# First norm, pooling, attention outputs and the order of the attention groups, changed together in a diffusion trunk kernel

## The chip, the cores and the metric

One core of a Trainium2 chip runs the whole program. The metric is the device time of one execution in microseconds (us); a profile is one more execution, taken with the hardware profiler. TensorE does the matrix products and transposes, VectorE, ScalarE and GpSimd the rest, and SP does nothing but issue transfers between DRAM and SBUF, in the order of its own list and waiting on semaphores. VectorE is DVE in the rows, ScalarE ACT, GpSimd POOL, TensorE PE, and its weight loads PEld.

## The reference

A step of a diffusion backbone of two layers, on 128 context tokens and 1024 latent tokens of width 1024. What the change touches lies in layer 0, up to its output projection. In short:

```python
ada = silu(cond) @ w_ada[l] + b_ada[l]            # per layer; cond is c (latent) or c_ctx (context)
sh1, sc1, g1, sh2, sc2, g2 = split(ada, 6)
u = layer_norm(x) * (1 + sc1) + sh1
proj = u @ w_in                                   # q: 8 heads of 64, k and v: 2 heads, p: 512 channels
q, k = rms_norm(q, q_g), rms_norm(k, k_g)         # rotary on the latent tokens
attn = block_attention(q, k, v)                   # context reads context; latent reads latent and cached keys
pool = pool_mixer(p, w_pool, pool_scale)          # per group: (centred mean over 2/4/8/16 tokens - p) @ w_pool
x = layer_norm(alpha * x + g1 * (concat(attn, pool) @ w_out), ln_g, ln_b)
u = layer_norm(x) * (1 + sc2) + sh2
f = conv_ffn(u, w_up, conv, w_down)
x = layer_norm(alpha * x + g2 * f, ln_g, ln_b)
```

Layer 1 has a convolution and a Fourier mixer instead of attention and pooling.

## The kernel before

Every engine's list is written out by hand, and semaphores (named in `wait_ge` and `then_inc`) set the order between engines. Values that go into matrix products are kept in two parts, a rounded high part (made by ScalarE, `copy`, L870) and the rest as a low part (made by VectorE, `lo`, L1357, a subtraction); a product is three passes. The 1152 tokens are nine tiles of 128, the first of them the context. `act_a` and `act_b` hold activations with channels on the partitions.

**The modulation vectors (w_ada).** Each layer's 6 x 1024 columns are cut into halves of 512, *blocks*; `ada_half` (L89) says which block is which. Blocks 0 to 12 are early, 13 to 23 late. SP loads an early block in four pieces of 512 KB into the six slots of `ada_w` (`ada_units`, L463, each piece waiting for its slot's `ada_used`), `ada_block` (L1860) multiplies it with the conditions. Blocks 0 to 3 go to `ada_top` by ScalarE (`top_evac`, L889), and `top_cols` (L1885) turns them into the first shift and scale (`cols`). Blocks 4 to 12 go to `ada_row` by VectorE (`ada_evac`, L1401), and GpSimd stores them to DRAM (L748 to L756). Late blocks come through `late_w` (`late_units`, L473; the fifth piece waits for the ninth z_rdy), `late_block` on TensorE (L1870), `late_evac` on ScalarE (L894) and the same loop of stores on GpSimd.

**First norm, "in".** `ln_steps` (L393) runs eleven steps, each of them with tile s - 1 in its normalisation and tile s - 2 in its rounding. VectorE's step (`ln_vec`, L1409): statistics, reciprocal, the split of `act_a` (which raises act_rdy), `ada_evac` of block 4 + s. ScalarE's step (`ln_act`, L913): eight `ln_u` activations that apply shift and scale to the transposed tile (L939), the square root (L952), `ln_z` = normalised tile (L968), the copy to `act_a` (`rounding`). TensorE's step (`ln_turns`, L2016): block 4 + s, then eight transposes of `ln_z` into banks 6 and 7 (`ln_turn`), and ahead of tile 5's the first pooling product `chunk(0, 0)` (L2007). There is one `ln_z`, so the normalising of a tile waits for the transposes of the one before. SP (`ln_loads`) loads x three tiles ahead into `ln_y`, each behind z_rdy of the tile that leaves its slot.

**SP's order.** Blocks 0 to 2; two units of the pooling weights (`u_unit`, into `raw_u`, split later to `uw`); block 3; three tiles of x; block 4; two more units of raw_u; two of wq (`d_unit`, through `raw_d`); blocks and x of the norm; block 13; `bias_rows` (L485), which waits for `ada_stored` and for the ninth act_rdy and then reads the stored rows back; then wq, late blocks and wkv in turn.

**Pool projection and pooling.** TensorE runs `pool_chunk` for four groups and three thirds (`NCH` 3), with late blocks between them; results go to `pp`. GpSimd pools the four windows over it (L758 to L785), each a chain of passes over 1173 columns, after all of `bank_free` and after `brow_mm` 6.

**q, k, v.** `qkv` (L2055) of the nine tiles, with `turn_keys` (L2067) for the keys of each tile, which waits for VectorE's rotated k. The mixer product, `mix` (L2083), has 12 parts in three banks, each evacuated by `mix_out` on ScalarE; the first three stand ahead of the last tile's `turn_keys`, the others between the first group's peaks.

**Attention.** `Group` (L409) n is one tile of queries with one kv head; groups 0 and 1 are the context's (one block of keys, one turn of scores), 2 to 17 the sample's (nine blocks, three turns). Group n + 1's maxima are prepared while group n's scores run: `turn_queries`, four `peak_scores` (three matmuls of 384 columns each for a sample group, one of 128 for a context group), VectorE's `maximum`, `turn_peaks`. Then `scores`, ScalarE's exponentials and rounding, GpSimd's p_low (L814), and `weigh_high` and `weigh_low` into bank 6 + n % 2. Outputs: `outputs` copies the sums (ScalarE), four `o_inverse` (VectorE), `o_scale` (L1545) writes the scaled outputs from the bank to `o_f` and raises o_mul, `o_round` (ScalarE) and `o_split` (L1554, raises m_att) put them into `act_b`. `weigh_high` of group n waits for o_mul of group n - 2, whose bank it takes. Behind the last group come `wo`'s parts (`wo_hi`, `wo_lo`), the low parts of the mixed channels (`mixed_lo`) and the gate rows (`mid_gate`, L1926).

## Time and profile before

| what | us |
|---|---|
| time, median of 3 runs | 2843.91 (2843.7 to 2844.75) |
| the profiled execution: its time | 2844.56 |
| the profiled execution: its span | 2843.0 |
| TensorE busy (matmuls) | 2680.5, 94% |
| TensorE's weight loads | 2386.7, 84% |
| VectorE busy | 1530.3, 54% |
| ScalarE busy | 921.4, 32% |
| GpSimd busy | 433.3, 15% |

The span runs from the first instruction to the last; the execution's own time has 1.56 us around it. TensorE is busy nearly all the time, but a busy share is an average over stages. By the trace the first norm ends at 123.3 us (the ninth act_rdy), the q/k/v stage runs from 210.7 to 304.7 us, the first scores start at 326.5 us, the attention's groups follow each other every 14 us, and the output projection starts at 575.3 us.

### The profile page before, as it was taken

How to read it: one execution, taken by the hardware profiler on the slowest of the kernel's cores; microseconds unless marked ns; L12 is line 12 of the kernel's file. 1: busy time of each engine (PE TensorE's matmuls, PEld its weight loads, DVE VectorE, ACT ScalarE, POOL GpSimd, SP SyncE). 2: the span in 40 equal slices, each digit the busy share in tenths (PEclk: the TensorE clock that was granted, in tenths of full speed). 3: DMA queues.
4: the chain of work that ended last, by engine and by line, in shares of the span. 5: the costliest groups of instructions: out<-in, count | busy, mean ns of one | idle time of the engine just before them, and what ended most of it. 6: DMA issues, size and time to landing. Idle time of an engine off the chain costs nothing.

```text
span 2843.0 us, 36166 instructions
## 1 busy us (share of the span) xinstructions
PE 2680.5 (94%) x13884; PEld 2386.7 (84%) x13884; DVE 1530.3 (54%) x2157; ACT 921.4 (32%) x1402; POOL 433.3 (15%) x258
## 2 busy tenths in 40 slices
PE   5698799999899999999997899999899999999997
PEld 1477577768899999999996899978899999999996
DVE  1315588856555555555557433247555555555557
ACT  2521377745322222222225511136322222222223
POOL 1116187825000000000006100014000000000003
PEclk6799899999999999999999899999999999999999
DMA  9770100022311111111012212122311111110112
GB/s 329 275 267 6 62 1 1 1 90 82 126 45 44 44 44 44 44 37 44 30 37 74 74 41 71 59 90 82 126 45 44 44 44 44 37 44 30 42 32 82
DMA packets 171518, 196.08 MB, mean 69 GB/s; under 512 B 7625, under 2 KB 125877, under 8 KB 171439
## 3 DMA queue, kind: packets, MB, share of 16 engines
q1 hardware_dynamic: 169748, 194.33, 20.7%
q8 instruction: 53, 0.87, 0.1%
q0 software_dynamic: 1280, 0.33, 0.1%
q10 hardware_dynamic: 411, 0.34, 0.0%
q14 instruction: 26, 0.21, 0.0%
HBM read 175.64 MB, written 19.33 MB: 69 GB/s over the span
## 4 chain that ended last, share of the span: by engine, by line
PE 84%; DVE 6%; ACT 4%; issue 2%; DMA 2%; POOL 1%; SPq 0%; ACTq 0%; POOLq 0%; DVEq 0%
PE ps L2011 47%; PE ps L2230 18%; PE ps L1978 5%; PE ps L1961 2%; PE ps L2121 1%; PE ps L2157 1%; ACT ln_u L939 1%; PE ps L2142 1%; PE ps L2143 1%; PE ps L2063 1%; PE ps L2164 1%; DVE stats L1391 1%; DMA ada_w<-in_w_ada 1%; DVE small L1538 1%; PE ps L1923 1%
## 5 line engine op out<-in xcount | busy, mean ns | idle before, releaser
L2011 PE MATMUL ps<-act_b,uw 128*128 128x384 f32 x4608 | 808.0, 338 | 7.7 <-DVE act_b L1357 6.2
L2011 PEld LDWEIGHTS ps<-act_b,uw 128*128 128x128 f32 x4608 | 804.2, 189 | 9.5 <-DVE act_b L1357 6.8
L2011 PEld LDWEIGHTS ps<-act_a,uw 128*128 128x128 f32 x3456 | 605.2, 190 | 17.5 <-issue 9.2
L2011 PE MATMUL ps<-act_a,uw 128*128 128x384 f32 x3456 | 611.7, 339 | 6.8 <-DVE act_a L1357 5.3
L2230 PE MATMUL ps<-dw,hh 128*128 128x512 f32 x2112 | 502.7, 398 | 9.0 <-DVE acc L1651 9.0
L2230 PEld LDWEIGHTS ps<-dw,hh 128*128 128x128 f32 x2112 | 398.1, 189 | 108.7 <-DVE acc L1651 10.1
L1651 DVE TENSOR_TENSOR acc<-acc,ps 128x512 f32<-128x512 f32 x360 | 245.7, 686 | 215.1 <-PE ps L2230 215.1
L870 ACT ACTIVATE fa<-ps 128x384 f32<-128x384 f32 (+2 forms) x176 | 67.3, 410 | 839.0 <-PE ps L2011 839.0
L1357 DVE TENSOR_TENSOR uw<-raw_u,uw 128x1024 fp32r<-128x1024 f32 x112 | 136.6, 1221 | 121.3 <-ACT uw L870 118.0
L1612 DVE TENSOR_SCALAR ft<-fa,fgrp 128x1153 f32<-128x1153 f32 x44 | 38.7, 880 | 299.2 <-ACT fa L870 284.1
L814 POOL TENSOR_TENSOR p_low<-p_exp,p_top 128x1536 fp32r<-128x1536 f32 (+1 forms) x50 | 170.7, 3418 | 75.8 <-ACT p_top L870 75.3
L1681 DVE TENSOR_TENSOR fh<-ft,ps 128x384 f32<-128x384 f32 (+2 forms) x176 | 73.9, 450 | 168.4 <-PE ps L2011 160.7
L853 POOL TENSOR_TENSOR acc<-acc,gb_end 128x1024 f32<-128x1024 f32 x9 | 21.3, 2375 | 822.0 <-ACT acc L1217 822.0
L870 ACT ACTIVATE uw<-raw_u 128x1024 fp32r<-128x1024 f32 x112 | 117.8, 1053 | 66.3 <-PE ps L2011 66.2
L846 POOL TENSOR_SCALAR acc<-acc,stats 128x1024 f32<-128x1024 f32 x9 | 10.8, 1198 | 806.5 <-DVE stats L1399 806.5
L870 ACT ACTIVATE hh<-fh 128x384 fp32r<-128x384 f32 x132 | 66.5, 520 | 205.6 <-DVE fh L1681 205.6
L827 POOL TENSOR_TENSOR ln_y<-ln_y,gbm 128x1024 f32<-128x1024 f32 x18 | 43.5, 2417 | 424.3 <-ACT ln_y L948 424.3
L939 ACT ACTIVATE ln_u<-ps,cols 128x128 f32<-128x128 f32 x216 | 78.3, 467 | 87.9 <-PE ps L1923 77.7
L1538 DVE TENSOR_REDUCE small<-ps 128x1 f32<-128x1152 f32 (+1 forms) x72 | 88.5, 1230 | 15.2 <-PE ps L2121 13.4
L1196 ACT ACTIVATE ft<-ft 128x1153 f32<-128x1153 f32 x44 | 51.5, 1171 | 132.7 <-DVE ft L1614 126.8
L1068 ACT ACTIVATE p_exp<-ps 128x1536 f32<-128x1536 f32 (+1 forms) x50 | 71.0, 1421 | 38.8 <-PE ps L2143 38.8
L1357 DVE TENSOR_TENSOR hh<-fh,hh 128x384 fp32r<-128x384 f32 x132 | 73.2, 555 | 17.4 <-ACT hh L870 11.9
(208 smaller groups left out, 3135.9 us busy)
## 6 DMA issues: line engine op xcount, KB each, us to landing
raw_u<-in_w_up SPq DMA_DIRECT2D x88, 512.0 KB, 4.0
ada_w<-in_w_ada SPq DMA_DIRECT2D x52, 512.0 KB, 6.5
late_w<-in_w_ada SPq DMA_DIRECT2D x44, 512.0 KB, 6.5
raw_d<-in_w_down SPq DMA_DIRECT2D x44, 512.0 KB, 3.7
raw_u<-in_w_in_odd SPq DMA_DIRECT2D x20, 512.0 KB, 3.8
ln_y<-in_x_all SPq DMA_DIRECT2D x18, 512.0 KB, 5.1
xs<-ln_y SPq DMA_DIRECT2D x18, 512.0 KB, 2.6
acc<-xs SPq DMA_DIRECT2D x6, 1536.0 KB, 11.6
```

The costliest lines, as they stand in the source:

```text
L814: gp.tensor_tensor(p_low[:, s % 3, 0:nb, :], p_exp[:, s % 2, 0:nb, :], p_top[:, s % 3, 0:nb, :].bitcast(F32), ALU.subtract).then_inc(p_lo, 1)
L870: return act.activation(o, i, ACT.Copy)
L939: o = act.activation(ln_u[:, k * P:(k + 1) * P], ps[:, 6 + k // 4, (k % 4) * P:(k % 4 + 1) * P], ACT.Identity, bias=cols[:, l, c0, k, cc:c ...
L1068: act.activation(p_exp[:, s % 2, 0:nb, :], ps[:, 3:3 + nb, :], ACT.Exp).then_inc(exp_done, 1)
L1357: return v.tensor_tensor(dst, src, hi.bitcast(F32), ALU.subtract)
L1538: v.tensor_reduce(g.peak(h), ps[:, 0:nb, 0:nw], mybir.AxisListType.XY, ALU.max, negate=True).then_inc(mx_done, 1)
L1651: return v.tensor_tensor(a, a, ps[:, 6 + j % 2, :], ALU.add).then_inc(down_added, 1)
L1681: o = v.tensor_tensor(f_h[l][:, s0:s0 + ln], f_t[l][:, p0:p0 + ln], ps[:, 3 + c, s0 - c * CH:s0 - c * CH + ln], ALU.mult)
L1961: mm = pe.matmul(ps[:, 2 * tile + h, :], src[:, k, a, tile * P:(tile + 1) * P], wo[l][:, k, w, 512 * h:512 * (h + 1)], start=n == 0 and (a ...
L1978: mm = pe.matmul(ps[:, 2 * (tile % 3) + h, :], src[:, k, a, tile * P:(tile + 1) * P], wo[l][:, k, w, 512 * h:512 * (h + 1)], start=(k, a, ...
L2011: mm = pe.matmul(out, uw[:, u_slot, w, k, :], src[:, k, a, c * CH:(c + 1) * CH], start=(k, w, a) == (0, 0, 0), stop=(k, w, a) == (KD - 1, ...
L2230: mm = pe.matmul(ps[:, 6 + h, :], hh[l][:, b, a, tile * P:(tile + 1) * P], w_[:, b, w, 512 * h:512 * (h + 1)], start=(b, a, w) == (0, 0, 0 ...
```

## The change

**Group order.** Places 0, 1, 2 hold groups 2, 0, 1; from place 3 on nothing moves. Slots and banks go by place. `outputs()` is the half of the group's bank in which the scaled outputs are kept.

```diff
-            def __init__(self, g):
+            def __init__(self, place):
+                g = (2, 0, 1)[place] if place < 3 else place
                 self.g, self.kv, self.ctx, self.q = g, g % 2, g < 2, g // 2 - 1
                 self.nk = 1 if self.ctx else LKB
                 self.key0 = LAT + PAST if self.ctx else 0
                 self.sizes = [1] if self.ctx else [TRI] * (LKB // TRI)
-                self.s0 = g if self.ctx else 2 + (g - 2) * (LKB // TRI)
+                self.s0 = (0, LKB // TRI, LKB // TRI + 1)[place] if place < 3 else 2 + (place - 2) * (LKB // TRI)
                 self.last = len(self.sizes) - 1
-                self.slot = g % 2
-                self.bank = 6 + g % 2
+                self.slot = place % 2
+                self.bank = 6 + place % 2
...
+
+            def outputs(self):
+                return ps[:, self.bank, :].rearrange("p (a h t) -> p a h t", h=2, t=P)[:, :, self.kv, :]
```

**First norm, loads.** x of the first three tiles comes between the first blocks, the blocks 11 and 12, two units of raw_u and two of wq behind the norm's loads; block 4 + tile stands behind its tile's transposes, and the halves that the blocks 4 to 10 hold are exchanged. The x load of tile + 3 waits for the transposes (zt_done) and no longer for z_rdy; so does late block 13's fifth piece.

```diff
+MIX_EARLY = 7
...
-    if m < 7:
-        return 1, m - 4
-    if m < 13:
-        return 0, m - 3
-    return (1, 3) if m == 13 else (0, m - 4) if m < 16 else (1, m - 12)
+    if m == 4:
+        return 1, 0
+    if m < 11:
+        return 0, m - 1
+    return (1, m - 10) if m < 14 else (0, m - 4) if m < 16 else (1, m - 12)
...
-    return {s: [4 + s] for s in range(9)} if kind == "in" else {}
+    return {s: [s + 2] for s in range(2, 11)} if kind == "in" else {}
...
-        ada_row = at("ada_row", [P, 3, 512], F32, off_s + 28672)
+        ada_row = at("ada_row", [P, 6, 512], F32, off_s + 24576)
+        ada_side = at("ada_side", [P, 3, 512], F32, off_s + 12288)
```
```diff
-                        sp.wait_ge(z_rdy, NT)
+                        sp.wait_ge(zt_done, NT)
...
+            def first_x(s):
+                sp.dma_start(ln_y[:, s, :], dram_rows(t["x_all"], s)).then_inc(x_ld[s], 16)
+
+            ada_units(0)
+            ada_units(1)
+            first_x(0)
+            ada_units(2)
+            ada_units(3)
+            first_x(1)
+            first_x(2)
+            ada_units(4)
             for n in range(2):
                 u_unit(n, u_source(n))
-            ada_units(3)
-            for s in range(3):
-                sp.dma_start(ln_y[:, s, :], dram_rows(t["x_all"], s)).then_inc(x_ld[s], 16)
-            ada_units(4)
...
-                            sp.wait_ge(z_rdy, tile + (NT * i4 + 1))
+                            sp.wait_ge(zt_done if i1 is None else z_rdy, tile + (NT * i4 + 1))
...
-                        for m in ada_steps(kind).get(3 + j, []):
-                            ada_units(m, i)
+                        if i1 is None:
+                            ada_units(5 + j, i)
...
-            for n in range(2, 4):
-                u_unit(n, u_source(n))
-            for k in range(2):
-                d_unit(D_QKV + k, t["w_in_even"][0][k * P:(k + 1) * P, 0:AW], AW)
             ln_loads("in", t["x_all"])
+
             def wq_unit(k):
                 d_unit(D_QKV + k, t["w_in_even"][0][k * P:(k + 1) * P, 0:AW], AW)
+
+            ada_units(11)
+            ada_units(12)
+            u_unit(2, u_source(2))
+            u_unit(3, u_source(3))
+            wq_unit(0)
+            wq_unit(1)
```

**First norm, ScalarE and VectorE.** The normalised tile is written over `ln_y`; there is no `ln_z` in it. The copy to `act_a` stands ahead of the normalising; the normalising of a tile and the rounding of the tile two before share a step.

```diff
-            ln_act("in", act_a)
+            def first_norm(s):
+
+                if s.live(2):
+                    tile = s.tile(2)
+                    cc = 1 if s.first(2) else 0
+                    if s.first(2):
+                        act.wait_ge(cols_done, 2)
...
+                    for k in range(KD):
+                        o = act.activation(ln_u[:, k * P:(k + 1) * P], ps[:, 6 + k // 4, (k % 4) * P:(k % 4 + 1) * P],
...
+                st, y = stats[:, s.slot(0), :], ln_y[:, s.slot(0), :]
+                if s.live(0):
+                    act.wait_ge(stat2, s.tile(0) + 1)
+                    act.activation(st[:, 34:35], st[:, 33:34], ACT.Sqrt, bias=eps, scale=1.0).then_inc(sd2, 1)
+                if s.live(2):
+                    tile = s.tile(2)
+                    act.wait_ge(mod_done, tile + 1)
+                    copy(act_a[:, :, 0, bass.ds(tile * P, P)], ln_u[:].rearrange("p (k t) -> p k t", k=KD)).then_inc(act_hi, 1)
+                if s.live(0):
+                    act.wait_ge(rs2, s.tile(0) + 1)
+                    act.activation(y, y, ACT.Identity, bias=st[:, 36:37], scale=st[:, 35:36]).then_inc(z_rdy, 1)
+                if s.i is None and s.base == 0:
+                    top_evac(2)
+                    top_evac(3)
+                elif s.i is None and s.base == 2:
+                    for n in range(2):
+                        u_hi_at(n, 0, n)
+
+            ln_steps(act, first_norm)
 
```
```diff
+                used = ADA_SLOTS + 4 * m + 4
                 v.wait_ge(ada_used, used if i is None else i * 12 + used)
-                if turn:
-                    v.wait_ge(ada_st[slot], 32 * turn if i is None else i * 32 + 32 * turn)
-                v.tensor_copy(ada_row[:, slot, :], ps[:, 3 + m % 3, :]).then_inc(ada_bank, 1)
+                if i is not None:
+                    row = ada_row[:, bass.ds(i * 3 + (m - 5), 1), :].rearrange("p a n -> p (a n)")
+                else:
+                    row = ada_side[:, (4, 11, 12).index(m), :]
+                v.tensor_copy(row, ps[:, 3 + m % 3, :]).then_inc(ada_bank, 1)
...
+            def first_norm(s):
+
+                if s.live(0):
+                    tile, st = s.tile(0), stats[:, s.slot(0), :]
+                    v.wait_ge(x_ld[s.slot(0)], s.third(0) * 16 + 16)
+                    norm_stats(ln_y[:, s.slot(0), :], st, 20).then_inc(stat2, 1)
+                    v.wait_ge(sd2, tile + 1)
+                    norm_scale(st, 20).then_inc(rs2, 1)
+                for m in ada_steps("in").get(s.base, []):
+                    ada_evac(m, s.i)
+                if s.live(2):
+                    tile = s.tile(2)
+                    v.wait_ge(act_hi, tile + 1)
+                    lo(act_a[:, :, 1, bass.ds(tile * P, P)], ln_u[:].rearrange("p (k t) -> p k t", k=KD), act_a[:, :, 0, bass.ds(tile * P, P)]).then_inc(act_rdy, 1)
+                if s.i is None and s.base < 2:
+                    cols_of(range(s.base, s.base + 1))
+                elif s.i is None and s.base == 2:
+                    u_lo_at(0, 0, 0)
+                    u_lo_at(1, 0, 1)
...
-                    o = v.tensor_tensor(o_f[HD * odd:HD * odd + HD, :, :],
+                    o = v.tensor_tensor(g.outputs()[HD * odd:HD * odd + HD],
...
-                lo(act_b[:, blocks, 1, cols_], o_f[:], act_b[:, blocks, 0, cols_]).then_inc(m_att, 1)
+                lo(act_b[:, blocks, 1, cols_], g.outputs(), act_b[:, blocks, 0, cols_]).then_inc(m_att, 1)
```

**Rows and pooling.** GpSimd stores the early rows only (there is a row buffer for each); ScalarE issues the stores of the late rows. Each pooling window starts with its own group's `bank_free`; only the last waits for `brow_mm` 6.

```diff
+                l, half = ada_half(m)
                 e = m - ADA_LATE
                 act.wait_ge(ada_used, ADA_SLOTS + 4 * m + 4)
                 if e >= 2:
                     act.wait_ge(late_st[e % 2], 32 * (e // 2))
                 copy(late_row[e % 2][:], ps[:, 6 + m % 2, :]).then_inc(ada_bank, 1)
+                act.wait_ge(ada_bank, m + 4)
+                for c in range(2):
+                    act.dma_start(ada[l, c::2, half * 512:half * 512 + 512], late_row[e % 2][c::32, :]).then_inc(late_st[e % 2], 16)
...
-            for m in range(ADA_TOP):
+            for m in range(2):
                 top_evac(m)
-            for n in range(2):
-                u_hi_at(n, 0, n)
```
```diff
-            for m in range(ADA_TOP, ADA_ALL):
+            for m in range(ADA_TOP, ADA_LATE):
                 l, half = ada_half(m)
+                rows = ada_side[:, (4, 11, 12).index(m), :] if m in (4, 11, 12) else ada_row[:, m - 5, :]
                 gp.wait_ge(ada_bank, m + 4)
-                if m < ADA_LATE:
-                    rows, done = ada_row[:, (m - ADA_TOP) % 3, :], ada_st[(m - ADA_TOP) % 3]
-                else:
-                    rows, done = late_row[(m - ADA_LATE) % 2][:], late_st[(m - ADA_LATE) % 2]
...
+                    gp.dma_start(ada[l, c::2, half * 512:half * 512 + 512], rows[c::32, :]).then_inc(ada_st[(m - ADA_TOP) % 3], 16)
+
+            gp.wait_ge(u_split, 2 + U_FFN0)
             for g, w in enumerate(WINDOWS):
 
+                gp.wait_ge(bank_free[g % 2], 3 * (g // 2 + 2))
+                if g == NPG - 1:
+                    gp.wait_ge(brow_mm, 6)
+                    for a in range(2):
+                        o = gp.memset(vv[:, :, a, 1, :].bitcast(F32), 1.0 - a)
+                    o.then_inc(v_one, 1)
```

**Mixer and TensorE.** Seven mixes stand ahead of the last tile's `turn_keys`, with their `mix_out` on ScalarE ahead of the last tile's k rounding. `weigh_high` and the first gate wait for m_att.

```diff
             pe.wait_ge(setup_c, 2)
-            for m in range(ADA_TOP):
-                ada_block(m)
-            top_cols()
+            for n in range(2):
+                ada_block(2 * n)
+                ada_block(2 * n + 1)
+                top_cols(n)
+            pe.wait_ge(cols_done, 2)
...
+                z = ln_z if i4 else ln_y[:, tile % 3, :]
                 pe.wait_ge(z_rdy, NT * i4 + tile + 1)
...
-                    mm = pe.transpose(ps[:, 6 + k // 4, (k % 4) * P:(k % 4 + 1) * P], ln_z[:, k * P:(k + 1) * P], ident)
+                    mm = pe.transpose(ps[:, 6 + k // 4, (k % 4) * P:(k % 4 + 1) * P], z[:, k * P:(k + 1) * P], ident)
...
-                        pe.wait_ge(o_mul, NGR)
+                        pe.wait_ge(m_att, NGR)
...
-                for s in range(NT + 1):
-                    for m in ada_steps(kind).get(s, []):
-                        ada_block(m)
-                    if s == 6:
+            def first_turns(next_chunk):
+
+                for tile in range(NT):
+                    if tile == 5:
                         next_chunk(0)
-                    if s:
-                        ln_turn(s - 1, LN[kind]["i4"])
-                    if s == NT:
-                        next_chunk(1)
+                    ln_turn(tile, 0)
+                    ada_block(ADA_TOP + tile)
+                next_chunk(1)
...
-            for m in range(3):
+            for m in range(MIX_EARLY):
                 mix(m)
...
-                    pe.wait_ge(o_mul, n - 1)
+                    pe.wait_ge(m_att, n - 1)
...
             turn_queries(0)
-            mix(3)
             for h in range(G):
                 peak_scores(0, h)
-                mix(4 + 2 * h)
-                mix(5 + 2 * h)
+                mix(MIX_EARLY + h)
+            for m in range(MIX_EARLY + G, NPG * NCH):
+                mix(m)
```

On ScalarE `mix_out` moves into the last tile of `qkv_tile` (`MIX_EARLY` of them), the last two tiles leave the loop, and `o_round` reads `g.outputs()`.

## Rows read from the trace of the kernel before

**Rows 1.** Windows by stage: stretch, us, busy us (x instructions), clock, DMA share, GB/s.
```profile
123.30:210.70 87.40, 78.60 (x481) 57.91 (x473) 10.34 (x17) 19.20 (x38) 12.37 (x22) 0.91 0.81 281
210.70:305.00 94.30, 84.92 (x452) 72.86 (x452) 54.35 (x103) 15.60 (x51) 47.42 (x45) 0.92 0.02 6
361.50:558.00 196.50, 195.32 (x911) 156.26 (x910) 169.48 (x169) 152.61 (x141) 156.72 (x69) 1.00 0.00 1
```
**Rows 2.** The same windows over three stretches of the first norm.
```profile
0.00:16.00 16.00, 4.92 (x24) 1.54 (x28) 0.00 (x0) 3.43 (x5) 4.29 (x6) 1.00 0.70 229
16.00:98.40 82.40, 54.84 (x280) 23.58 (x272) 25.73 (x56) 35.19 (x71) 8.05 (x14) 0.67 1.02 360
108.00:124.00 16.00, 10.29 (x52) 8.82 (x56) 6.94 (x12) 12.41 (x27) 1.12 (x2) 0.63 0.03 9
```
**Rows 3.** Waits of SP's queue up to 130 us: total us, times, longest us.
```profile
SPq L488 <- DVE act_a L1357: 22.2, 1, 22.2
```
**Rows 4.** Timeline of ScalarE and VectorE, a turn of the norm loop: start, us, instruction.
```profile
95.57 0.68 DVE L1407 COPY ada_row<-ps 128x512 f32<-128x512 f32 x1
...
96.32 2.90 ACT L939 ACTIVATE ln_u<-ps,cols 128x128 f32<-128x128 f32 x8 [2.15 <-PE ps L1923]
...
99.89 1.24 ACT L968 ACTIVATE ln_z<-ln_y,stats 128x1024 f32<-128x1024 f32 x1 [0.48 <-DVE stats L1399]
...
103.58 2.90 ACT L939 ACTIVATE ln_u<-ps,cols 128x128 f32<-128x128 f32 x8 [1.51 <-DVE act_a L1357]
```
**Rows 5.** DMA issues: count, KB each, median us from issue to landing.
```profile
ada_parts<-ada_row POOLq DMA_DIRECT2D x18, 8.0 KB, 4.9
```
**Rows 6.** Waits of TensorE from 124 to 305 us.
```profile
PE ps L2072 <- DVE k L1357: 9.4, 5, 4.4
...
PE ps L1881 <- DMA late_w<-in_w_ada: 7.4, 4, 4.0
```
**Rows 7.** Timeline of TensorE in the first norm.
```profile
90.97 4.44 PE L2011 MATMUL ps<-act_a,uw 128*128 128x384 f32 x24
```
**Rows 8.** GpSimd and VectorE in time from 246 us, and a group of instructions by form.
```profile
246.82 7.43 POOL L772 TENSOR_TENSOR pool_t<-pool_t 128x1173 f32<-128x1173 f32 x3
...
249.24 2.49 DVE L1503 TENSOR_TENSOR xn<-xn,g_row 128x512 f32<-128x512 f32 x1
...
L1503 DVE TENSOR_TENSOR xn<-xn,g_row 128x512 f32<-128x512 f32 x5 | 3.4, 681 | 0.0
```
**Rows 9.** The windows once more, behind TensorE's longest wait for k.
```profile
258.00:263.50 5.50, 5.50 (x19) 4.79 (x20) 2.78 (x7) 1.62 (x5) 3.18 (x2) 0.54 0.06 15
```
**Rows 10.** Timeline of TensorE, from the first query transposes to the third group's weighing.
```profile
314.82 1.09 PE L2108 MATMUL ps<-con,q_two 128*128 128x128 f32 x4 [0.61 <-ACT kt L870]
...
326.48 0.47 PE L2142 MATMUL ps<-q_top,kt 128*128 128x512 f32 x1 [0.50 <-ACT q_low L870]
...
346.66 0.76 PE L2142 MATMUL ps<-q_top,kt 128*128 128x512 f32 x1
...
361.49 0.39 PE L2142 MATMUL ps<-q_top,kt 128*128 128x512 f32 x1
...
367.48 1.56 PE L2157 MATMUL ps<-p_top,vv 128*128 128x512 f32 x6
```
**Rows 11.** Timeline of VectorE in the attention, its start and its end.
```profile
338.38 1.36 DVE L1538 TENSOR_REDUCE small<-ps 128x1 f32<-128x1152 f32 x1
...
339.65 0.94 DVE L1543 RECIPROCAL o_inv<-o_raw 64x128 f32<-64x128 f32 x1
...
362.41 1.72 DVE L1357 TENSOR_TENSOR act_b<-o_f,act_b 128x256 fp32r<-128x256 f32 x1
...
569.04 3.76 DVE L1357 TENSOR_TENSOR act_b<-o_f,act_b 128x256 fp32r<-128x256 f32 x1 [2.29 <-ACT act_b L870]
```
**Rows 12.** Timeline of GpSimd at the end of the attention.
```profile
565.59 6.93 POOL L814 TENSOR_TENSOR p_low<-p_exp,p_top 128x1536 fp32r<-128x1536 f32 x2 [0.17 <-ACT p_top L870]
```
**Rows 13.** Groups of VectorE's instructions by form, 361 to 558 us: busy us, mean ns, idle.
```profile
L1357 DVE TENSOR_TENSOR q_low<-ps,q_top 64x512 fp32r<-64x512 f32 x14 | 9.6, 682 | 2.6 <-ACT q_top L870 1.8
```

More of the change, by code:

```diff
@@ L1043, in _ @@
             qkv_tile(0, 0, True)
-            with act.Fori(0, NQ // 2) as i:
+            with act.Fori(0, NQ // 2 - 1) as i:
                 for j in range(2):
                     qkv_tile(i * 2 + (j + 1), 1 - j, False)
+            qkv_tile(NQ - 1, 1, False)
+            qkv_tile(NQ, 0, False, last=True)
             def q_round(n):
@@ L1444, in step @@
                         lo(dest[:, :, 1, bass.ds(tile * P, P)], ln_u[:].rearrange("p (k t) -> p k t", k=KD), dest[:, :, 0, bass.ds(tile * P, P)]).then_inc(act_rdy, 1)
-                    for m in ada_steps(kind).get(s.base, []):
-                        ada_evac(m, s.i)
                 def loop(i):
@@ L1456, in from_psum, with first_loop @@
                 return 2, ps[:, 2 * slot:2 * slot + 2, :]
-            ln_vec("in", act_a, None)
+            def first_norm(s):
[16 more added lines that the diff above has]
+                    u_lo_at(1, 0, 1)
+            def first_loop(i):
+                if i is None:
+                    chain.leave(2)
+                else:
+                    chain.enter(i, 6)
+            ln_steps(v, first_norm, first_loop)
             for n in range(NPG):
@@ L2095, in mix @@
                 mm.then_inc(mix_done, 1)
-            for m in range(3):
+            for m in range(MIX_EARLY):
                 mix(m)
```

75 lines of the change are left out of this document (27 added, 48 removed).

## Prediction

> **What bounds the kernel now.** I read the windows by stage first, to see which engine fills each stretch. From 361.5 us the groups run with TensorE busy 195.3 of 196.5 us [rows 1]; the work after the attention is untouched. So what VectorE, ScalarE or GpSimd save in the attention's steady part is worth nothing, and only the stretch before 361.5 us and the seam behind the attention can move the end. Next come the windows of the transfers. The queue is full from 16 us on: by 98.4 us it has moved 33.3 MB (16 x 0.229 + 82.4 x 0.360), and from 108 to 124 us it stands almost still [rows 2]. The waits of SP say why: 22.2 us for the last split of act_a [rows 3]. That is `bias_rows`, which waits for the ninth act_rdy (123.3 us); all later loads are queued behind it on SP. And act_rdy is late because a turn of the norm loop takes 7.26 us, from the first ln_u of a tile (96.32) to that of the next (103.58), with ln_z (1.24 us), the copy to act_a and its split one after the other [rows 4]. Then the pool stage has TensorE busy 78.6 of 87.4 us, and the q/k/v stage 84.9 of 94.3 [rows 1], of which 9.4 us are waits for VectorE's k [rows 6].
>
> **Part 1, the first norm (up to q/k/v).** Removed: the single ln_z. The norm is written back into ln_y, so ScalarE's copy to act_a comes ahead of the next normalising, and VectorE's split runs beside that. Of the 7.26 us the 1.24 us of ln_z and some 0.3 us of handover leave the chain: about 5.7 us a tile. That is less than the 7.3 us that a tile's loads need (four pieces of w_ada and one tile of x, 2.62 MB, at 0.360 MB/us [rows 2]). So the transfers are late next, and the sum goes by bytes. The last act_rdy now needs what stands ahead of its split in VectorE's list, ada_evac(12), and so all 13 early blocks: 27.3 MB of w_ada, 4.7 MB of x, 1.0 MB of raw_u and 0.4 MB of constants, 33.4 MB together. The queue of before has moved that at 98.4 us; the other two units of raw_u, two of wq and the four pieces of block 13 now come behind it. One hole is new: x(tile+3) waits on SP for the transposes of its tile, and TensorE does `chunk(0, 0)`, 4.44 us [rows 7], ahead of tile 5's. Queued on SP behind that wait are x8, the blocks 10 to 13, raw_u and wq. I charge 3 us, between nothing (pieces in flight cover it) and 4.4. Block 12 is through TensorE about 1 us after landing, at 102.4. Its copy (0.68 us [rows 4]) and GpSimd's store, which lands 4.9 us after its issue [rows 5], let SP pass `ada_stored` at about 109; the act_rdy, a copy and a split behind the block, is earlier and no longer decides. Against 123.3 that is -14.3 us.
>
> The pool stage behind it is the same list on TensorE, and TensorE is its bound, so it moves as a whole. Its 7.4 us of waits for late_w [rows 6] stay: block 14 is still asked for after `bias_rows`. Two costs are added. The 22 stores of the late rows are issued by ScalarE behind its own late_evac; the copies of wq, wkv and pp are queued behind them, and ScalarE is busy 19.2 of 87.4 us [rows 1]: nothing to 1 us. And GpSimd's windows 0 to 2 now run beside VectorE's splits of wq and wkv. A two-operand instruction took 2.49 us beside GpSimd where its kind takes 681 ns undisturbed [rows 8]; the loads of wkv and of block 22 are queued on SP behind such splits. Bounds 0 and 5 us, for up to three that meet a pass; I take 1.3 for both additions, near to one blocked instruction, since the splits are few. Part 1: **-13 us**, between -18 (no hole, rows stored in time) and -6 (the larger additions and a second hole).
>
> **Part 2, q/k/v.** The pooling leaves this stage except for window 3, which still waits for bank 1 and brow_mm and ends some 18 us into the stage (three of its passes are the 7.43 us [rows 8]). VectorE's rotation of the first tiles then runs alone. Of the 9.4 us of waits [rows 6] the first keeps about 1 us (the chain of the cached keys) and the rest, some 0.2 us each, another 1: 7.4 go. Behind the longest wait the granted clock is 0.54 from 258 to 263.5 us [rows 9], (1 - 0.54) x 5.5 = 2.5 us lost, and I put 1 us to the shorter ones. That makes 10.9; the end of window 3 may still touch the first tile: **-10**, between -6 and -12.5.
>
> Here a rule is weighed. The row shows q_low<-ps, whose first operand is in PSUM, at 682 ns beside GpSimd through the whole attention [rows 13], while instructions with two SBUF operands stand still for whole passes. The Trainium skill, "SBUF — State Buffer", section Who interferes with whom, has the same split as a rule: the port pair is an exclusive lock, the second comer blocks fully, and an instruction with at most one SBUF input stays out of it. It speaks against the move of the pooling: what the lock cost in q/k/v it can cost in the pool stage. By the rule with every such split late the sum would be the second rival's, by the rows of before, whose pool stage has no GpSimd arithmetic, the forecast.
>
> **Part 3, the mixer and the order of the groups.** Seven mixes instead of three fill TensorE's wait for the last tile's k; ScalarE evacuates them ahead of that tile's k_round, on which the last keys wait, and has time for it: nothing. Five mixes are left, but the first four peaks are now a full group's. From the first transposes (314.82) to the first scores (326.48) it was 11.7 us [rows 10]. A full head's reduction takes 1.36 us [rows 11] and its three matmuls stand in the open, so by estimate each head takes 0.85 us more: 15.1 us, +3.4. Then three groups. Before, from 326.48 over 346.66 to 361.49 [rows 10], 35.0 us: two short groups with one full set of peaks in the open, 20.2, and a full group, 14.8. Now: a full group over short peaks, held by GpSimd's p_low (two are 6.93 us [rows 12]), 13; a short group whose maxima alternate with four reciprocals of 0.94 us [rows 11] and wait for the full group's last p_low, 10; a short group with the next full peaks in the open, 14 of the 20.2. 37 us, +2. The order exposes one more set of full peaks. With half clock behind the waits I take **+6**, between -1 (only the saved mixes count) and +9.
>
> **Part 4, outputs in their bank.** o_f goes; o_scale writes PSUM and o_split reads it. In the steady part VectorE saves about a microsecond a group, which TensorE hides. Added is that the bank is free at m_att, not at o_mul: `weigh_high` two groups on waits for o_round and o_split, and the peaks, scores and weights behind it on TensorE with it. The split (362.41, 1.72 us [rows 11]) is 3.3 us ahead of that weigh_high (367.48 [rows 10]): 0. At the seam the split at 569.04 stands 3.76 us [rows 11] beside GpSimd's last p_low; read from PSUM it doesn't. But mixed_lo, next on VectorE and with two SBUF operands, meets the same p_low, so only the split's own time comes off: **-0.4**, between 0 and -1.7. The gate behind k = 2 waits for m_att too; the split stands right behind the wo_lo that k = 2 needs: 0.
>
> **Sum.** -13 - 10 + 6 - 0.4 = -17.4 us on the profiled execution's 2844.56: 2827.2. The median of the runs is 0.65 lower: **2826.5**.
>
> **Rivals.** First: the order costs nothing. For it speaks that mixes fill the full peaks' gaps, against it that five mixes are fewer than the nine of before. Part 3 is 0: 2820.5. Second: the lock moves. Windows 0 to 2 meet the splits of wq and wkv, SP is held, late blocks 22 and 23 come late; part 1 is -6: 2833.5. For it speaks the 2.49 us row, against it VectorE's 10.3 busy us in the 87.4 [rows 1]. Third: the stores don't hold SP and no hole comes; part 1 is -18: 2821.5. Fourth, on the other side: the queue runs dry in every tile, since x(tile+3) now waits for TensorE's transposes and all blocks stand behind it. Where each of the five x loads other than the chunk's loses 4.4 us, 22 us are added: 2848.5; it is a loss from 3.5 us a load. Against it speaks that a tile's chain (5.7 us) is shorter than its bytes (7.3). Fifth, the same sign: the later release of the bank stops TensorE. If m_att comes 2 us behind `weigh_high` in 14 groups, 28 us are added: 2854.5; it decides from 1.2 us a group, beyond the 3.3 us of slack.
>
> **How the numbers follow.** Chances: forecast 0.47, first rival 0.20, second 0.12, third 0.12, fourth 0.05, fifth 0.04. About 0.2% (5.7 us) is what a measurement of this kernel can tell from no change. Faster by more (under 2838.2) are the forecast, the first, the third and most of the second rival: 0.88. Same: the edges of the forecast and of the second, 0.06. Slower: the rest, 0.06. The range goes from 2812 (parts 1 to 3 at -18, -12.5 and -1) to 2838 (part 1 at -6 with part 3 at +9 and part 2 at -9), which leaves the last two rivals out.
>
> **What the profile after would show.** Right: the ninth act_rdy at about 105, SP held by the stores and not by act_a, q/k/v from about 198 us, no wait for k over 1.5 us in it, the fourth group's scores some 17 us ahead of 361.5, groups still 14 us apart. Wrong: a queue with holes in every tile before 100 us, splits of wq or wkv of over 2 us, weigh_high idle for act_b, or the first scores less than 13 us behind the first transposes.

## The result and the profile after

The changed kernel takes 2826.76 us (median of 5 runs, 2819.72 to 2829.55), against 2843.91 before: a ratio of 0.9936, 95% interval 0.9921 to 0.995 (it is estimated from all runs of both kernels; the two medians alone give 0.994). The forecast was 2826.5. The total hides that two of its parts were off, in opposite directions. The table reads the traces by stage. Each border is the start of a row of the timeline: SP's read of the stored rows, the first q/k/v product, the keys of the last tile but one, the first query transposes, and the gate behind the third part of the output projection. The profiled execution of each kernel stands in it; the experiments in its lower rows are told below.

| kernel | read of rows at | to q/k/v | q/k/v | last keys | transposes to gate | gate to end |
|---|---|---|---|---|---|---|
| before | 123.34 | 87.35 | 94.00 | 10.13 | 272.95 | 2255.2 |
| after | 110.09 | 91.53 | 81.88 | 9.74 | 276.88 | 2255.0 |
| e1 order of before | 109.69 | 87.94 | 82.11 | 9.76 | 270.91 | 2255.0 |
| e2 pooling late | 110.65 | 85.58 | 93.16 | 9.74 | 276.30 | 2255.5 |
| e3 o_f back | 110.42 | 91.30 | 82.39 | 9.74 | 275.81 | 2253.1 |
| e4 block 13 ahead | 111.98 | 90.11 | 82.08 | 9.74 | 275.44 | 2253.4 |
| e5 context last | 108.67 | 90.55 | 83.29 | 9.94 | 270.33 | 2253.1 |
| e6 block 22 ahead | 112.64 | 85.83 | 82.08 | 9.75 | 276.67 | 2258.3 |
| e7 half blocks | 101.61 | 90.59 | 82.08 | 9.74 | 275.74 | 2253.3 |
| e8 e5 and e6 | 111.02 | 84.32 | 82.04 | 9.74 | 270.00 | 2255.4 |
| e9 e8 and the seam | 110.41 | 85.26 | 82.07 | 9.75 | 265.59 | 2253.0 |

Rows whose code is the same in a column show how far one execution stands from the next: 108.7 to 112.6 in the first column (before and e7 aside), 87.9 to 91.5 in the pool stage (after, e1, e3 and e5), 81.9 to 82.4 in q/k/v (e2 aside, and with e5 up to 83.3), 2253.0 to 2258.3 behind the gate, 275.4 to 276.9 from the transposes to the gate in the six with the changed order. A difference of a microsecond says something in the last keys, one of two in q/k/v and from the transposes to the gate; in the other columns one execution can't tell less than four or five. The medians of one kernel have the same scatter in them, so the experiments are judged by the stage that they touch, and by the ratio to the kernel before.

The windows of the changed kernel, in the columns of [rows 1]: the transfers up to 98.4 us, the pool stage, q/k/v.

```profile
16.00:98.40 82.40, 55.18 (x304) 26.15 (x296) 32.97 (x73) 48.70 (x97) 8.59 (x15) 0.75 0.99 354
110.09:201.62 91.53, 81.37 (x481) 59.85 (x481) 14.17 (x15) 19.20 (x36) 30.13 (x30) 0.89 0.77 271
201.62:283.50 81.88, 80.40 (x450) 68.90 (x449) 47.98 (x103) 15.50 (x51) 15.64 (x14) 0.98 0.03 7
```

The queue runs at 354 GB/s where it ran at 360 [rows 2]: by this rate the new waits of SP for transposes cost, as an estimate, 82.4 x (1 - 354/360) = 1.4 us of transfers. The last piece of block 12 came in at 101.6 all the same, 3.2 us behind 98.4: with units of raw_u and wq beside it the queue had moved 33.9 MB by then (101.6 x 0.334), not 33.4. The pool stage has 30.1 us of GpSimd in it where it had 12.4 [rows 1], all of that the issuing of stores, and VectorE is busy 3.8 us longer with the same 15 to 17 instructions. The q/k/v stage lost 31.8 us of GpSimd, and TensorE idles 1.5 us in it where it idled 9.4.

The ninth act_rdy is the split at 103.82; block 12 passes TensorE behind a wait for its last piece. The timeline of TensorE and VectorE:

```profile
101.59 1.43 PE L1926 MATMUL ps<-ada_w,conds 128*32 128x512 f32 x8 [2.03 <-DMA ada_w<-in_w_ada]
...
103.82 1.23 DVE L1398 TENSOR_TENSOR act_a<-ln_u,act_a 128x1024 fp32r<-128x1024 f32 x1
```

SP then stands for the store of block 12's row, and later for the splits of wq, as its waits from 108 us show (total us, times, longest us):

```profile
SPq L588 <- DVE wq L1398: 6.3, 2, 4.1
SPq L493 <- DMA ada_parts<-ada_side: 6.1, 1, 6.1
```

What [rows 3] showed, 22.2 us of SP before the last split of act_a, is gone; the store took its place with 6.1 us. TensorE's waits for k in the q/k/v stage, 9.4 us in [rows 6], fell to 1.4:

```profile
PE ps L2129 <- DVE k L1398: 1.4, 3, 1.1
```

In TensorE's timeline the rows that answer to [rows 10] are the first transposes at 293.24, the first scores at 307.20 and the fourth group's at 344.40 (314.82, 326.48 and 361.49 before):

```profile
293.24 1.03 PE L2165 MATMUL ps<-con,q_two 128*128 128x128 f32 x4 [0.56 <-ACT kt L878]
...
307.20 0.47 PE L2199 MATMUL ps<-q_top,kt 128*128 128x512 f32 x1 [0.34 <-ACT q_low L878]
...
344.40 0.77 PE L2199 MATMUL ps<-q_top,kt 128*128 128x512 f32 x1
```

### The profile page after: what moved, and what is told of

Its sections match the earlier page's. It is cut to its first block, busy times and chain, and to the rows that moved or that the text cites. A ratio compares the mean times of both kernels' runs of the same rounds, so it can differ in the third digit from the quotient of the medians.

```text
span 2825.1 us, 36154 instructions
## 1 busy us (share of the span) xinstructions
PE 2675.1 (95%) x13884; PEld 2384.5 (84%) x13884; DVE 1510.2 (53%) x2157; ACT 920.7 (33%) x1402; POOL 421.1 (15%) x236
## 4 chain that ended last, share of the span: by engine, by line
PE 82%; DVE 7%; ACT 4%; DMA 3%; issue 3%; POOL 1%; SPq 0%; ACTq 0%; POOLq 0%; DVEq 0%
PE ps L2072 47%; PE ps L2287 18%; PE ps L2039 5%; DMA ada_w<-in_w_ada 2%; DVE small L1598 2%; PE ps L2022 1%; PE ps L2120 1%; DVE stats L1428 1%; PE ps L2178 1%; ACT p_exp L1117 1%; PE ps L2199 1%; PE ps L2200 1%; DMA late_w<-in_w_ada 1%; PE ps L2221 1%; PE ps L1984 1%
## 5 line engine op out<-in xcount | busy, mean ns | idle before, releaser
L854 POOL TENSOR_SCALAR acc<-acc,stats 128x1024 f32<-128x1024 f32 x9 | 10.8, 1201 | 806.6 <-DVE stats L1436 806.6
L1603 DVE RECIPROCAL o_inv<-o_raw 64x128 f32<-64x128 f32 x72 | 67.1, 938 | 31.3 <-ACT o_raw L878 30.6
L1398 DVE TENSOR_TENSOR hh<-fh,hh 128x384 fp32r<-128x384 f32 x132 | 73.3, 555 | 17.4 <-ACT hh L878 12.0
## 6 DMA issues: line engine op xcount, KB each, us to landing
acc<-xs SPq DMA_DIRECT2D x6, 1536.0 KB, 12.4
```

What stands on the lines that cost most here:

```text
L1398: return v.tensor_tensor(dst, src, hi.bitcast(F32), ALU.subtract)
L1603: v.reciprocal(o_inv[g.out, cols_], o_raw[g.sum, cols_]).then_inc(inv_done, 1)
```

## The experiments

All are edits of the changed kernel.

**e1, the order of the groups as before.**

```diff
-                g = (2, 0, 1)[place] if place < 3 else place
+                g = place
-                self.s0 = (0, LKB // TRI, LKB // TRI + 1)[place] if place < 3 else ...
+                self.s0 = g if self.ctx else 2 + (g - 2) * (LKB // TRI)
```

> The changed kernel with the attention groups in the order of before (the two of the context first); seven early mixes and the rest stay. Theory (the order costs, because a full group's four peaks stand in the open twice): the first peaks are short again, so first transposes to first scores falls from 13.96 us to some 9 (four mixes fewer than before in it, where it was 11.7), and the first three groups from 37.2 to 35.0: about -7 us on the changed kernel's 2826.8, 2820. Rival (the order is free, since mixes fill the peaks and the short groups are held by p_low anyway): 2826 to 2828. Against both: if the sample's group first hides more than it shows, it is slower, 2830.

Measured: 2821.45 us, ratio 0.9924 (0.9909 to 0.9938). The first transposes to the first scores take 10.32 us:

```profile
289.50 0.63 PE L2165 MATMUL ps<-con,q_two 128*128 128x128 f32 x4 [0.57 <-POOL q_two L810]
...
299.82 0.47 PE L2199 MATMUL ps<-q_top,kt 128*128 128x512 f32 x1 [0.51 <-ACT q_low L878]
```

That is 3.6 us less than in the changed kernel, and from the transposes to the gate it is 6.0 us less (270.91 against 276.88; the five other kernels with the changed order have 275.4 to 276.7). The order costs; that it is free, the first rival, falls. Up to the start of the projection, ahead of a seam that is not the same in all of them (see e3), e1 takes 258.4 us and the six with the changed order 264.2 to 265.9. Against before (272.95) e1, with the early mixes alone, is 2.0 us shorter; so of part 3 the order is +5 to +7 and the mixes some -2, from one execution of e1 and of before.

**e2, the pooling windows behind the last bank and the columns, as before.**

```diff
             gp.wait_ge(u_split, 2 + U_FFN0)
+            gp.wait_ge(bank_free[0], 3 + 6)
+            gp.wait_ge(bank_free[1], 3 + 6)
+            gp.wait_ge(brow_mm, 6)
```

> The changed kernel with all four pooling windows where they were before, behind the last bank and the fifth and sixth columns. Theory (the port lock costs in both stages): q/k/v goes from 81.9 us back to about 94 (waits for k of 8 to 9 us, half clock behind the longest), and the pool stage, from the read of the stored rows (110.0) to the first q/k/v product (201.6), falls from 91.6 to about 89, because the splits of wq at 150 and 172 us (3.23 and 4.34 us for two) run undisturbed at 1.3 and block 22 is asked for 3 us earlier: +9, 2836. Rival (the late blocks are late because ScalarE issues the stores, not because of the lock): the pool stage stays at 91.6, +12, 2839.

Measured: 2834.64 us, ratio 0.9965 (0.9954 to 0.9975). The q/k/v stage is back at 93.2 us, with 10.8 us of waits for k, and the pool stage falls to 85.6. Here are the last two splits of wq and GpSimd's passes beside them (VectorE and GpSimd in time), TensorE's waits for block 22, and the window of the 32 products behind the second of these waits, first in the changed kernel:

```profile
171.04 4.69 POOL L780 TENSOR_TENSOR pool_t<-pool_t 128x1173 f32<-128x1173 f32 x2
...
171.94 4.34 DVE L1398 TENSOR_TENSOR wq<-raw_d,wq 128x512 fp32r<-128x512 f32 x2 [18.75 <-ACT wq L878]
...
182.42 1.06 PE L1941 MATMUL ps<-late_w,conds 128*32 128x512 f32 x8 [2.30 <-DMA late_w<-in_w_ada]
185.76 1.94 PE L1941 MATMUL ps<-late_w,conds 128*32 128x512 f32 x8 [2.28 <-DMA late_w<-in_w_ada]
...
185.70:193.49 7.79, 7.73 (x32) 5.85 (x32) 0.00 (x0) 0.60 (x1) 0.00 (x0) 0.67 0.89 321
```

then with the pooling late, and its row of SP's waits for wq:

```profile
173.31 1.29 DVE L1401 TENSOR_TENSOR wq<-raw_d,wq 128x512 fp32r<-128x512 f32 x2 [21.22 <-ACT wq L881]
...
182.03 1.06 PE L1944 MATMUL ps<-late_w,conds 128*32 128x512 f32 x8 [0.51 <-DMA late_w<-in_w_ada]
184.57 1.07 PE L1944 MATMUL ps<-late_w,conds 128*32 128x512 f32 x8 [1.47 <-DMA late_w<-in_w_ada]
...
184.57:189.93 5.36, 5.36 (x32) 4.27 (x32) 0.00 (x0) 0.60 (x1) 0.00 (x0) 1.00 1.03 374
...
SPq L588 <- DVE wq L1401: 3.2, 2, 3.0
```

Two splits that take 4.34 us together beside GpSimd take 1.29 without it, and SP's wait for wq falls from 6.3 to 3.2 us. ScalarE issues the late stores in both kernels, so it is the pooling, not the stores, that adds these 3.1 us. The pool stage pays 2 to 6 us for it (after, e1, e3, e4 and e5: 87.9 to 91.5, against 85.6), where I expected 2.6. By the Trainium skill, "SBUF — State Buffer", section Who interferes with whom, the shared port pair is an exclusive lock. By that rule two-operand splits had to stand still for GpSimd's passes here as they did in q/k/v, and these rows agree.

The waits for block 22 are 4.6 us in the changed kernel (3.8 to 5.0 in the six with the early pooling and block 22 behind wkv) and 2.0 here. The low clock comes on top: the 32 products behind the second wait have a granted clock of 0.67 and take 7.8 us (6.8 to 8.3 in the six), where they take 5.4 at 1.00 here. The last 32 small matmuls, 5.5 us at 0.65 against 3.7 at 1.00, don't follow the wait: in e1, with waits of 3.8 us, they take 3.7, and in e9, with none, 5.3.

**e3, outputs in SBUF again.**

```diff
-                    o = v.tensor_tensor(g.outputs()[HD * odd:HD * odd + HD],
+                    o = v.tensor_tensor(o_f[HD * odd:HD * odd + HD, :, :],
...
-                    pe.wait_ge(m_att, n - 1)
+                    pe.wait_ge(o_mul, n - 1)
```

> The changed kernel with the outputs in SBUF again (o_f, and o_mul where m_att was waited for). Theory (the bank pays at the seam alone): the steady groups stay at 14.0 us, the split of the last but one group stands beside GpSimd's p_low again (3.7 us instead of 0.42) and the gate behind the third part of the output projection comes 1.6 us later: 2828.4. Rival (the later release of the bank costs TensorE in the groups): the stretch from the fourth group to the projection falls from 214.8 us to 213.8 and the time is 2826 or below.

Measured: 2824.42 us, ratio 0.9932 (0.992 to 0.9945); transposes to gate 275.81. VectorE's groups by form over the steady groups (busy us, mean ns, idle), first of the changed kernel, then of this one:

```profile
L1398 DVE TENSOR_TENSOR act_b<-ps,act_b 128x256 fp32r<-128x256 f32 x16 | 6.5, 408 | 2.7 <-ACT act_b L878 2.7
```

```profile
L1399 DVE TENSOR_TENSOR act_b<-o_f,act_b 128x256 fp32r<-128x256 f32 x16 | 29.1, 1821 | 2.8 <-ACT act_b L879 2.8
```

The split is 1.4 us shorter from the bank, 22.6 us of VectorE in all, and the stage is not: neither theory holds at its price. The 1.6 us that the trace shows between the projection's start and the gate (10.95 against 12.51 before) are not the bank's, since e1 has the outputs in the bank and takes 12.54, and e3 has them not and takes 11.03. What changes is which products get the low clock. The windows of the first 24 and the next 12 products, in the changed kernel and then in e1:

```profile
559.17:566.54 7.37, 7.37 (x24) 5.60 (x24) 7.26 (x9) 0.84 (x3) 0.00 (x0) 0.77 0.76 257
567.16:570.10 2.94, 2.94 (x12) 2.17 (x12) 2.94 (x4) 2.17 (x4) 0.00 (x0) 1.00 0.95 308
```

```profile
547.87:553.63 5.76, 5.76 (x24) 4.43 (x24) 5.73 (x6) 0.19 (x1) 0.00 (x0) 1.00 0.69 207
555.87:560.40 4.53, 4.53 (x12) 3.20 (x12) 4.43 (x5) 3.75 (x5) 0.00 (x0) 0.62 0.98 320
```

In e1 the first part runs at the full clock, TensorE then waits 2.24 us for the third part's weights, and the products behind that wait have a granted clock of 0.62, between TensorE's two levels of 1.2 and 2.4 GHz (0.5 and 1.0), so the low one held for most of their time. In the changed kernel the low clock falls on the first part, the wait is 0.62 us, and the products behind it have the full clock. The order of the groups does not decide it either: e6, with the order and the bank of the changed kernel, has the rows of e1 at the seam, and 12.4 us to the gate (TensorE's timeline):

```profile
554.58 5.76 PE L2022 MATMUL ps<-wo,act_b 128*128 128x512 f32 x24 [1.38 <-DVE wo L1398]
562.58 4.46 PE L2022 MATMUL ps<-wo,act_b 128*128 128x512 f32 x12 [2.24 <-DVE wo L1398]
```

Why the clock falls earlier in one execution than in another stays open; all of them stood idle for the same 1.4 us before.

**e4, block 13 ahead of raw_u and wq.**

```diff
             ada_units(12)
+            late_units(13)
             u_unit(2, u_source(2))
...
-            late_units(13)
             bias_rows(range(2, 4), ADA_LATE)
```

> The changed kernel with late block 13 loaded right behind block 12, ahead of two units of raw_u and two of wq. Theory (the pool stage starts with TensorE waiting for it): the two waits of 1.75 and 1.49 us at 110 us go, with the half clock behind them, and all of the stage moves forward: -3 to -4, 2823. Rival (TensorE meets the next late transfer anyway, as the queue gives the same bytes in another order, or ScalarE stands before a wq copy that now comes later): 2826.8, with longer waits for blocks 14 to 17.

Measured: 2826.19 us, ratio 0.995 (0.9937 to 0.9963), pool stage 90.1 us. In the changed kernel TensorE waits twice for block 13 and once for block 14; here it waits for block 14 alone, for about as long (TensorE's timelines).

```profile
110.33 1.07 PE L1941 MATMUL ps<-late_w,conds 128*32 128x512 f32 x8 [1.75 <-DMA late_w<-in_w_ada]
112.88 1.94 PE L1941 MATMUL ps<-late_w,conds 128*32 128x512 f32 x8 [1.49 <-DMA late_w<-in_w_ada]
...
122.31 1.07 PE L1941 MATMUL ps<-late_w,conds 128*32 128x512 f32 x8 [1.49 <-DMA late_w<-in_w_ada]
```

```profile
121.21 1.94 PE L1941 MATMUL ps<-late_w,conds 128*32 128x512 f32 x8 [5.55 <-DMA late_w<-in_w_ada]
123.80 1.94 PE L1941 MATMUL ps<-late_w,conds 128*32 128x512 f32 x8 [0.66 <-DMA late_w<-in_w_ada]
```

The rival holds: 4.7 us of waits became 6.2. Where the next loads come behind the stored rows, another order of what is loaded before only moves the wait.

**e5, the context's groups last.**

```diff
-                g = (2, 0, 1)[place] if place < 3 else place
+                g = (place + 2) % NGR
-                self.s0 = (0, LKB // TRI, LKB // TRI + 1)[place] if place < 3 else ...
+                self.s0 = place * (LKB // TRI) if not self.ctx else (NGR - 2) * (LKB // TRI) + g
...
-                        pe.wait_ge(m_att, 2 * SIDE)
+                        pe.wait_ge(m_att, NGR)
```

> The changed kernel with the sixteen groups of the sample first and the two of the context last (the first parts of the output projection then wait for all outputs). Theory (what the order costs is the sets of full peaks that stand in the open; there are two of them in the changed order, and here only the first group's is left, since nothing is prepared beside the last group): one set beside a short group, some 14.6 us for a group that needs 4 to 5 of its own, comes off, the last short group has no peaks beside it, and the seam behind it waits for a p_low of 1.3 us and not of 3.5: the stretch from the first scores to the gate behind the third part of the projection falls from 262.9 us to about 252, 2816. Rival (TensorE fills the open peaks with something, or the output chain of the last two short groups, four reciprocals, is too long to hide): no gain or a loss of up to 3 us, 2827 to 2830.

Measured: 2822.51 us (2816 expected), ratio 0.9925 (0.9913 to 0.9938); first scores to gate 255.3 us, where 252 were expected and the changed kernel has 262.9. The open set of peaks is gone, but part of the gain is spent before the projection:

```profile
551.29 8.38 PE L2022 MATMUL ps<-wo,act_b 128*128 128x512 f32 x24 [7.07 <-DVE wo L1398]
```

**e6, block 22 ahead of wkv.**

```diff
             late_units(21)
+            late_units(22)
             wkv_unit(0)
             wkv_unit(1)
-            late_units(22)
             late_units(23)
```

ScalarE's copies of the two units come behind the first third of the last group.

> The changed kernel with late block 22 loaded ahead of the first two units of wkv, and ScalarE's copies of these one step later. GpSimd's passes and VectorE's blocked splits of wq stay. Theory (the lock costs through SP, which stands before wkv for the splits of wq, 6.3 us, while block 22 is queued behind): the waits for blocks 22 and 23 (2.30 and 2.28 us in the changed kernel) fall to 2 us together and the stage from the read of the rows to the first q/k/v product from 91.5 to about 88: -3, 2823. Rival (late blocks come by the queue's bytes, as with block 13 ahead): the waits only move to block 23, 2827; or wkv is split too late for the first q/k/v product: slower.

Measured: 2826.6 us, ratio 0.993 (0.9914 to 0.9946): by the total not to be told from the changed kernel. By the stage it is: 85.8 us here, and 84.3 and 85.3 in e8 and e9, which have the same edit, against 87.9 to 91.5 without. Counted from the start of the span, q/k/v begins at 198.5, 195.3 and 195.7 us in these three, and at 197.6 to 202.1 in the five without. The splits of wq still stand for GpSimd (4.13 us for two); TensorE waits for neither half of block 22 now, and 1.58 us for the second half of block 21 (the 2.30 and 2.28 us that the expectation gives to blocks 22 and 23 were the two halves of block 22). In TensorE's timeline, block 21's second half and block 22:

```profile
180.47 1.07 PE L1941 MATMUL ps<-late_w,conds 128*32 128x512 f32 x8 [1.58 <-DMA late_w<-in_w_ada]
...
185.83 1.92 PE L1941 MATMUL ps<-late_w,conds 128*32 128x512 f32 x16
```

With e2 this shows how the lock costs: through SP, which stands before wkv with a late block queued behind, and then through the low clock behind TensorE's wait. The gain does not show in the total: the six runs lie between 2814.95 and 2831.58, and in the profiled one the rows were read at 112.64 and the end came 2258.3 us behind the gate, in code that is the same.

**e7, half the bytes for blocks 5 to 10.**

```diff
-                    sp.dma_start(ada_w[:, a % ADA_SLOTS, :, :], w[u][:, :, bass.ds(col, 512)])...
+                    wide = 512 if i is None else 256
+                    sp.dma_start(ada_w[:, a % ADA_SLOTS, :, 0:wide], w[u][:, :, bass.ds(col, wide)])...
```

> The changed kernel with the pieces of the blocks 5 to 10 loaded at half their columns (the other half of the modulation rows comes from stale weights). Theory (the norm loop goes by bytes, 2.62 MB a tile): a tile now needs 1.57 MB, 4.4 us, so its own chain decides: from one tile's transposes to the next 5.7 us instead of 7.3, six tiles, the ninth act_rdy and the read of the stored rows some 10 us earlier. Rival (the chain over ScalarE, VectorE and TensorE decides already): 7.3 us stay.

Measured: the rows are read at 101.61, 8.5 us earlier. From the third tile's transposes to the ninth's it is 35.4 us, 5.9 a tile, where the changed kernel has 43.8, 7.3 a tile (53.74 to 97.50):

```profile
52.01 1.50 PE L1985 MATMUL ps<-con,ln_y 128*128 128x128 f32 x8
...
87.38 1.09 PE L1985 MATMUL ps<-con,ln_y 128*128 128x128 f32 x8
```

So the norm loop of the changed kernel goes by bytes. In e7 the chain over ScalarE decides: the first ln_u of one tile and of the next are 5.5 to 5.7 us apart, as in the prediction, and 7.0 over the tile that waits for `chunk(0, 0)`.

**e8, context last and block 22 ahead.**

> The changed kernel with the context's groups last and block 22 ahead of wkv. Both theories add, since they lie in different stages: 2813. If the one is true and the other not, 2816 or 2823.

Measured: 2816.77 us, ratio 0.9905 (0.9891 to 0.992). The pool stage is 84.3 us and the attention 270.0, so both gains are in their stages; the total lies 4 us behind the expectation.

**e9, and the seam.** ScalarE rounds the mixed parts 3 and 2 in the last group but one and the weights 7 and 6 in the last; VectorE's splits of them move with that.

```diff
+                if n == NGR - 2:
+                    mixed_hi(3)
+                    mixed_hi(2)
...
+                if n == NGR - 1:
+                    act.wait_ge(st_done, TURNS)
+                    wo_hi(0, 7, D_OUT0)
+                    wo_hi(0, 6, D_OUT0)
                 if n:
                     o_round(n - 1)
```

> The kernel of the run before (context last, block 22 ahead), with the seam behind the attention put in order for it: the two mixed parts that the projection reads first are rounded and split beside the last two groups, and the first two parts of its weights beside the last, where they stood behind the output chain of the last but one group. Theory (with the context last, TensorE stands 7.07 us before the projection because these are queued behind four reciprocals and ScalarE's rounding of that group): the projection starts some 4 us earlier and the stretch from the first query transposes to the gate behind its third part falls from 270.0 to about 266, 2813. Rival (the last group's own chain, reciprocals, scaling, rounding and split, sets the gate whatever comes ahead of it): the projection starts earlier, but waits before its third part, 2816 to 2817.

Measured: 2810.68 us, ratio 0.9887 (0.9871 to 0.9904), below the changed kernel's interval and the fastest of all. The wait before the projection is 3.0 us and there is none before its third part:

```profile
541.65 11.50 PE L2026 MATMUL ps<-wo,act_b 128*128 128x512 f32 x36 [3.04 <-DVE wo L1400]
```

## Why the prediction was right, point by point

**The read of the stored rows: right.** Block 12 was through TensorE at 103.0 (102.4 forecast), the ninth act_rdy at 105.05 (about 105), and SP passed the store at 110.09 (about 109); the store and not act_a decided, as said. The forecast's own terms give 108.0 there (102.4, 0.68 and 4.9), not 109; from the end of the copy to the read it was 6.3 us. The step that the sum goes by bytes was tested by e7. The hole was charged 3 us; the queue's rate gives 1.4, and the 0.5 MB loaded beside block 12 some 1.5 more. No run takes the parts of the new norm (no ln_z, the exchange of blocks, the order of loads) apart.

**The pool stage: mis-sized.** The term was +1.3 us for the stores by ScalarE and the blocked splits together, between 0 and 5. It measured +4.2 in the profile of after, +0.6 in e1, which has the same code there, and +3 to +4 in e3, e4 and e5. I took the price near one blocked instruction, "since the splits are few"; what counts is not how many there are but which wait on SP lies behind them, and whether TensorE's clock falls behind the wait. Both pairs of wq that met the windows were blocked (3.23 and 4.34 us for two, one split of 2.6 us in each, which was named as a sign of being wrong), and the second pair held block 22. That is the second rival's mechanism, at more than half of its price in this execution and at none in e1's. The stores by ScalarE cost nothing that shows: with them and the pooling late (e2) the stage is 85.6 us, with neither of the two (before) 87.4. Part 1 came to -9.1 us where -13 was forecast; q/k/v began at 201.6, not at about 198. In e1 the same part comes to -13.1.

**q/k/v: right, and under-sized.** -12.1 us against -10. The waits for k fell to 1.4 us where I left 2, and the granted clock of the stage rose from 0.92 [rows 1] to 0.98. In the windows TensorE's idle time fell by 7.9 us (7.4 forecast) and its busy time, for the same products at the higher clock, by 4.5 (3.5). I took 1 us off for the end of window 3 beside the first tiles; only one wait of 1.1 us is left of that. e2 gives 11.3 us for the move alone.

**The mixer and the order: right.** First transposes to first scores rose by 2.3 us (3.4 forecast), the three groups by 2.2 (2 forecast), and the last keys came 0.4 us sooner; the fourth group's scores stood 17.1 us ahead, as forecast. The rest of the +6 was for the low clock behind the waits. It is there: the granted clock is 0.50 over the open peaks of the third place (329.78 to 344.40), and the fourth group, at 0.89, takes 15.3 us and not 14.0, so that the projection starts 5.5 us later behind the first transposes than before (265.9 against 260.4). The stage up to the gate has only 3.9 us of it, because the seam was 1.6 us shorter in this execution; in e6, with the same code there, it was not. e1 shows that the order is the cost.

**The bank: right that it is worth next to nothing.** No row of weigh_high waits for act_b, so the fifth rival fell; the bank brings 1.4 us a group on VectorE, which TensorE hides. e3 does not tell its -0.4 from zero.

The fourth rival fell by the rate of the queue: SP waited 18.3 us for transposes (six waits), but pieces in flight covered all of it but 1.4. The third, "the stores don't hold SP", was wrong: they hold it 6.1 us.

The sum by stages is -13.2 + 4.2 - 12.1 - 0.4 + 3.9 - 0.2 = -17.8 on the span, against -17.4 forecast. That the total came within a microsecond is a cancelling, and partly luck: +1.1 at the read of the rows and +2.9 in the pool stage, against -2.1 in q/k/v and -2.1 in the order with its seam. The five runs lie between 2819.72 and 2829.55, too. The parts were good to some 3 us each, and no better.

## What to carry to other kernels

A GpSimd pass that is moved to another stage takes its port with it: look there not for how many two-operand instructions of VectorE it meets, but for the one behind which a transfer is queued, and put that transfer ahead of the wait (e6). In a pipelined chain of groups of unlike length, the cost of an order is the preparation that no long group covers; put the short groups where nothing is prepared beside them, at the end, and then see what the seam behind them queues for (e5 to e9). Where loads come by bytes, moving one block ahead only names another block as the late one (e4); in e6 the block stood behind a wait of SP, and there it helped.

## What the runs showed of the hardware

The low TensorE clock fell on different products of the same code from one kernel to the next (0.77 then 1.00 at the seam of the changed kernel, 1.00 then 0.62 in e1, 1.00 then 0.64 in e6, whose order and bank are the changed kernel's). In the pool stage the 32 small matmuls of the last columns took 5.55 us in the changed kernel and 3.73 in e1, behind the same wait of 0.72 us; that is half of the 3.6 us by which the two differ in this stage. No run here says what decides it.
